# The order of one engine around the last score block of a head, and a weight block that is loaded in two halves

## The chip, the cores and the metric

The kernel runs on one core of a Trainium2 chip. The metric is the device time of one execution in microseconds (us). The times before are the median of three runs; one further execution was profiled, and the trace that is read here is of that one.

## What is computed

One pre-norm decoder block on 528 tokens (16 learned meta tokens and 512 tokens), width 1024, in float32. Two mixers run on the same normalised input `u`: a gated linear recurrence (HGRN2) and a differential softmax attention. Each has 8 heads of width 128. Cut to what matters for this change:

```
proj = u @ w_in                       # 10 blocks of 1024 columns; 8 of them are split over 8 heads
hq, hf, hi, hz, aq, ak, av, az, ga, gb = split(proj)
oA = rmsnorm(hgrn2(hq, log f, 1 - f, hi)) * silu(hz)      # per head
p  = softmax(q1 k1^T / 8) - lam * softmax(q2 k2^T / 8)    # causal, in 4 blocks of 128 queries
oB = rmsnorm(p @ v) * silu(az)                            # per head
m  = sigmoid(ga) * (oA @ w_a) + sigmoid(gb) * (oB @ w_b)
out = rmsnorm(h + m @ w_out)
```

## The kernel before, in words

**Products in three passes.** A float32 product is made of three passes in a faster format: each operand is split into a high part and a rest, and TensorE adds high x high, rest x high and high x rest (`three`, L639 to L641). So each weight block that arrives in `w_raw` needs a high part `w_hi`, written by ScalarE (ACT), and a rest `w_lo`, written by VectorE (DVE) or, for some blocks, by ScalarE and a DMA that adds (issued from GpSimd, POOL).

**A head.** The 8 heads run one after the other; heads 0 to 6 have the same program, the last (head 7) differs at its end. TensorE walks 60 slots in a fixed order. Slots 0 to 31 are four "units" of 8 slots (columns HI, HZ, AV, AZ of `w_in` for this head). Slots 32 to 59 are two "pairs" `r = 0, 1` of seven "parts" `j = 0..6` (two slots each): a Strassen-like scheme makes, of weight blocks for the *next* head (HF and HQ, then AK and AQ), sums of halves (`sum_2`, `sum_4` on DVE, and two adding DMAs, `add_s1` and `add_s3`), and DVE combines the products (`sum_75`, `sum_16`, `out_21`, `out_22`, `out_12`). Between the slots lie the small products of this head's recurrence and attention, at places written out by hand (`HG_AT`, `AT_AT`): the scores of the last query block `s3` after slot 44, the turned (transposed) probabilities `t3` after slot 51 (L892, L895), the product with the values `a3` after slot 53 (L901, L902), and `turn` after slot 59 (L846).

**The last score block.** It goes PE `s3`, DVE `masked(3)` (L1728, L1735: mask, negate, row minimum), ACT `exps(3)` (L1147), DVE `probs(3)` (L1745 to L1747), PE `t3`, ACT `probs_out(3)`, PE `a3`.

**The end of a head.** ACT `square` (L1139) of what `a3` left, DVE `norm_sum(1)` (L1672, L1677), POOL `rstd_pow` (L592), DVE `norm(1)` (L1684), PE `turn`. Then DVE `sum_16(1)` (L1525) and `out_21(1)` (L1546, the first that writes `qT`); TensorE may start the next head's first unit only when `out_21(1)` is done, since it overwrites the bank that `out_21` reads (the wait on `comb` in `unit`). `opening(h + 1)` (L1450 to L1457) prepares the next head's recurrence, and `half_hi`, `half_lo` (L334, L339) split the next head's first weight block HI.

**Queues.** Every engine works its list in order; a wait at its head holds all that is behind it. SyncE (SP) issues all loads: HI into `w_raw[0]` when the last rest of pair 1 (`low(1, 6)`) is done, then HZ into `w_raw[1]`; AV into `w_raw[0]` waits for `lo_ready`, the second half of HI's rest. POOL issues the adding DMAs and makes the power of -1/2 (`rstd_pow`).

After the heads six "gate" pairs follow; the first needs `add_s1` and `add_s3` on blocks GA and GB that are loaded in head 7. `add_s3` is issued by POOL behind the last `rstd_pow`.

Of the kernel before, what the change touches and what calls it, by code (L numbers as in the profile page):

```python
# [26 lines left out]
P = 128  # L27
# [4 lines left out]
KT = D // P  # L32
# [18 lines left out]
BLK = 512  # L51
SLOTS = 8
RAW = 2
UNITS = 4
# [53 lines left out]
def build(nc, x, meta_tokens, norm_g, w_in, lb_logits, hg_norm_g, da_lambda, da_norm_g,  # L108
# [124 lines left out]
    x_loaded = [sem(f"x_loaded{i}") for i in range(CH)]  # L233
    xres_loaded, stored = sem("xres_loaded"), sem("stored")
    w_loaded = [sem(f"w_loaded{i}") for i in range(2 * RAW)]

    slot_free = sem("slot_free")
    hi_ready, lo_ready, w_used = sem("hi_ready"), sem("lo_ready"), sem("w_used")
    hi_first = sem("hi_first")
    sums, pair_hi, pair_lo = sem("sums"), sem("pair_hi"), sem("pair_lo")  # L240
    base_loaded = [sem(f"base_loaded{i}") for i in range(2)]
    s1_added, s3_added, adds_begun = sem("s1_added"), sem("s3_added"), sem("adds_begun")
# [86 lines left out]

    def half_hi(act, half, loads, free):  # L330

        act.wait_ge(w_loaded[0], 16 * loads)
        act.wait_ge(w_used, free)
        act.activation(blk(w_hi, half), w_raw[:, 0, half * BLK:(half + 1) * BLK], ACT.Copy)             .then_inc((hi_first, hi_ready)[half], 1)  # L334

    def half_lo(dve, half, ready):

        dve.wait_ge((hi_first, hi_ready)[half], ready)
        ins = dve.tensor_tensor(blk(w_lo, half), w_raw[:, 0, half * BLK:(half + 1) * BLK], blk(w_hi, half).bitcast(F32),  # L339
                                ALU.subtract)  # L340
        if half == 1:
            ins.then_inc(lo_ready, 1)

    def part_hi(act, q, j, r, loads, i, free):

# [75 lines left out]
    with block:  # L421

        @block.sync
        def _(sp):
# [4 lines left out]
            def columns(h, col, r):  # L429

                load(r, w_in[bass.ds(h + col // P, 1), :, :])

            def base_21(h, col, r):

                sp.dma_start(sum_at(r), w_in[bass.ds(h + col // P, 1), :, 0:BLK].rearrange("u p n -> p (u n)")) \
                    .then_inc(base_loaded[r // RAW], 16)
# [10 lines left out]
            def pair_of_head(h, r, h_next, cols):  # L447

                q = 2 * h + r
                if r == 0:  # L450
                    base_21(h_next, cols[1], 0)
                    sp.wait_ge(unit_added[1], 16 * h + 16)
                    sp.sem_inc(slot_free, 1)
                else:
                    sp.wait_ge(sums, 2 * q - 1)
                    sp.wait_ge(pair_lo, LOWS * (q - 1) + 3)
                    sp.sem_inc(slot_free, 1)
                    base_21(h_next, cols[1], 0)
                    sp.wait_ge(pair_lo, LOWS * q)
                    sp.sem_inc(slot_free, 1)  # L460
                columns(h_next, cols[0], 0)
                if r == 0:
                    sp.wait_ge(unit_added[2], 16 * h + 16)
                else:
                    sp.wait_ge(part_added[1], 16 * q)
                sp.sem_inc(slot_free, 1)
                columns(h_next, cols[1], 1)
# [24 lines left out]
            with sp.Fori(0, HEADS - 1) as h:  # L492
                units_of_head(h)
                pair_of_head(h, 0, h + 1, PAIRS[0])
                pair_of_head(h, 1, h + 1, PAIRS[1])
                sp.wait_ge(pair_lo, LOWS * 2 * (h + 1))
                sp.sem_inc(slot_free, 1)
                columns(h + 1, HI, 0)
                sp.wait_ge(part_added[1], 32 * h + 32)
                sp.sem_inc(slot_free, 1)  # L500
                columns(h + 1, HZ, 1)
# [134 lines left out]
        def _(pe):  # L636
# [56 lines left out]

            def unit(h, j, k):

                if k == 0:
                    if j == 0:
                        pe.wait_ge(lo_ready, UNITS + h + 1)
                        pe.wait_ge(c11_taken, 2 * h + 2)
                    else:  # L700
                        pe.wait_ge(unit_added[j - 1], 16 * h + 16)
                    if j < 2:
                        pe.wait_ge(comb, 10 * h + 8 + 2 * j)
                    elif j == 2:
                        pe.wait_ge(sec_taken, UNITS + 2 * h + 1)
                    else:
                        pe.wait_ge(gate_ready, 2 * h + 3)
                section(4 + j, j, [k])
# [295 lines left out]
        def _(act):  # L1004
# [137 lines left out]
            def exps(h, b):  # L1142
                act.wait_ge(nb_ready, 4 * h + b + 1)
                n = n_keys(b)
                for comp in range(2):
                    e, at_nb = (e1, e2)[comp][:, b % 2, 0:n], 2 * (b % 2) + comp
                    act.activation(e, e, ACT.Exp, bias=nb[:, at_nb:at_nb + 1], scale=-1.0,  # L1147
                                   accum_out=(l_1, l_2)[comp][:, b:b + 1]).then_inc(exp_done, 1)
# [23 lines left out]
            def head(h, last):  # L1172
# [15 lines left out]
                def p_1(r):  # L1188

                    save_p1(2 * h + r, made(h, 2 * UNITS + PARTS * r))  # L1190

                def p_5(r):

                    save_p5(2 * h + r, made(h, 2 * UNITS + PARTS * r + 1))

                def parts(r, *js):

                    for j in js:
                        part_of_head(h, r, j)
# [31 lines left out]
                c_11(0)  # L1231
                parts(1, 0, 3)
                probs_out(h, 2)
                parts(1, 1, 2, 4, 5)
                exps(h, 3)
                if last:
                    gate_rest(0, 2 * h)
                else:
                    act.wait_ge(comb, 10 + 10 * h + 5)
                    act.activation(kk[:, META + HALF:], kk[:, META + HALF:], ACT.Tanh, scale=0.5).then_inc(k_tanh, 1)  # L1240
                p_1(1)
                p_5(1)
                parts(1, 6)
                probs_out(h, 3)
                square(h, 1, B_A, at_done, atn(h, "a3"))
                c_11(1)
                if last:
                    gate_hi(0, 0, 3)
                else:
                    half_hi(act, 0, UNITS * h + 7, made(h, 16))  # L1250
                    half_hi(act, 1, UNITS * h + 7, made(h, 17))
                    unit_hi(act, 1, UNITS * h + 7, 1, made(h, 19), True)

# [83 lines left out]
        def _(dve):  # L1337
# [128 lines left out]
            def first_chain(ins):  # L1466
                first_mark(ins)
                dve.wait_ge(dve_own, first[0])

            opening(0, first_mark, first_chain)  # L1470
            dve.sem_inc(dve_own, OWN - first[0])

# [81 lines left out]
            def head(h, last):  # L1554
# [257 lines left out]
                sum_16(0)  # L1812
                out_21(0)
                out_22(0)
                low(1, 1, 2)
                sum_2(dve, 2 * h + 1, 0)
                out_12(0)
                masked(3)
                sum_4(dve, 2 * h + 1, 0)
                low(1, 5)  # L1820
                probs(3)
                low(1, 6)
                sum_75(1)
                if not last:
# [2 lines left out]
                if last:  # L1827
                    gate_low(0, 0, 3)
                else:
                    half_lo(dve, 0, h + 1)  # L1830
                    half_lo(dve, 1, UNITS * h + UNITS + 5)
                norm(1, B_A)
                sum_16(1)
                out_21(1)
                out_22(1)
                gated(1)
                out_12(1)
# [143 lines left out]
```

## Time and profile before

| | us |
|---|---|
| median of 3 runs | 736.97 (735.65 to 739.42) |
| profiled execution, its own time | 736.84 |
| its span, from the first to the last instruction | 735.0 |
| TensorE busy with matmuls | 707.4 (96%) |
| VectorE busy | 531.7 (72%) |
| ScalarE busy | 364.4 (50%) |
| GpSimd busy | 111.9 (15%) |
| mean granted TensorE clock | 0.997 of full |

The profiled execution took 1.84 us more than its span (736.84 - 735.0), and 0.13 us less than the median. Busy times are sums over all instructions of an engine. A row of a timeline gives start, duration, engine, line, operation, tiles and shapes, and in brackets how long the engine had been idle before it and what it waited for. Matmuls overlap: one is started each 0.12 us or so although one lasts 0.28, so a short stall shows as a wider step between two starts rather than as idle time.

### The profile page before, as it was taken

How to read it: one execution, taken by the hardware profiler on the slowest of the kernel's cores; microseconds unless marked ns; L12 is line 12 of the kernel's file. 1: busy time of each engine (PE TensorE's matmuls, PEld its weight loads, DVE VectorE, ACT ScalarE, POOL GpSimd, SP SyncE). 2: the span in 40 equal slices, each digit the busy share in tenths (PEclk: the TensorE clock that was granted, in tenths of full speed). 3: DMA queues.
4: the chain of work that ended last, by engine and by line, in shares of the span. 5: the costliest groups of instructions: out<-in, count | busy, mean ns of one | idle time of the engine just before them, and what ended most of it. 6: DMA issues, size and time to landing. Idle time of an engine off the chain costs nothing.

```text
span 735.0 us, 14431 instructions
## 1 busy us (share of the span) xinstructions
PE 707.4 (96%) x4953; PEld 651.5 (89%) x4953; DVE 531.7 (72%) x1240; ACT 364.4 (50%) x739; POOL 111.9 (15%) x134
## 2 busy tenths in 40 slices
PE   3999999999999999999999999999989999999995
PEld 2998999999899999899989999989889988888884
DVE  4899888788778778868868877887678872735352
ACT  5454653655564555376455555446466562222232
POOL 2011211221121121121112112112111000000000
PEclk9999999999999999999999999999999999999998
DMA  7355546547547555654754655565747553335102
GB/s 271 115 130 129 129 123 164 129 114 177 111 111 194 120 128 138 162 127 123 164 139 101 188 107 134 143 166 127 196 124 207 189 174 112 98 103 201 58 13 102
DMA packets 35955, 101.86 MB, mean 139 GB/s; under 512 B 4018, under 2 KB 4420, under 8 KB 35924
## 3 DMA queue, kind: packets, MB, share of 16 engines
q1 hardware_dynamic: 21204, 68.29, 26.6%
q0 software_dynamic: 14400, 32.51, 25.6%
q10 hardware_dynamic: 320, 0.66, 0.3%
q8 instruction: 18, 0.29, 0.2%
q14 instruction: 13, 0.11, 0.0%
HBM read 66.84 MB, written 2.10 MB: 94 GB/s over the span
## 4 chain that ended last, share of the span: by engine, by line
PE 77%; DVE 7%; issue 6%; DMA 5%; ACT 2%; POOL 1%; DVEq 0%; SPq 0%; POOLq 0%; ACTq 0%
PE ps L639 21%; PE ps L641 21%; PE ps L640 21%; PE ps L805 3%; DMA w_raw<-w_raw 3%; PE ps L875 2%; PE ps L791 1%; PE ps L901 1%; DMA w_raw<-in_w_in 1%; PE ps L892 1%; PE ps L821 1%; DVE e L1735 1%; DMA x_in<-in_x 1%; ACT e L1147 1%; DVE e L1747 1%
## 5 line engine op out<-in xcount | busy, mean ns | idle before, releaser
L639 PE MATMUL ps<-uT_hi,w_hi 128*128 128x272 f32 (+3 forms) x704 | 226.3, 321 | 0.8 <-ACT p L1117 0.8
L640 PE MATMUL ps<-uT_lo,w_hi 128*128 128x272 f32 (+3 forms) x704 | 215.5, 306 | 0.0
L641 PE MATMUL ps<-uT_hi,w_lo 128*128 128x272 f32 (+3 forms) x704 | 215.2, 306 | 0.0
L639 PEld LDWEIGHTS ps<-uT_hi,w_hi 128*128 128x128 f32 x704 | 133.2, 189 | 8.6 <-issue 1.2
L641 PEld LDWEIGHTS ps<-uT_hi,w_lo 128*128 128x128 f32 x704 | 133.0, 189 | 6.0
L640 PEld LDWEIGHTS ps<-uT_lo,w_hi 128*128 128x128 f32 x704 | 133.2, 189 | 4.5
L639 PE MATMUL ps<-t_hi,w_hi 128*128 128x256 f32 x352 | 103.1, 293 | 2.6 <-DVE w_lo L362 2.6
L641 PE MATMUL ps<-t_hi,w_lo 128*128 128x256 f32 x352 | 99.5, 283 | 0.0
L640 PE MATMUL ps<-t_lo,w_hi 128*128 128x256 f32 x352 | 99.4, 282 | 0.0
L321 ACT ACTIVATE w_hi<-w_raw 128x1024 fp32r<-128x1024 f32 x53 | 56.0, 1059 | 84.2 <-PE ps L641 54.7
L355 ACT ACTIVATE w_hi<-w_raw 128x512 fp32r<-128x512 f32 x132 | 78.5, 624 | 21.9 <-DMA w_raw<-w_raw 9.0
L362 DVE TENSOR_TENSOR w_lo<-w_raw,w_hi 128x512 fp32r<-128x512 f32 x100 | 67.1, 687 | 11.2 <-ACT w_hi L355 9.8
L328 DVE TENSOR_TENSOR w_lo<-w_raw,w_hi 128x1024 fp32r<-128x1024 f32 x29 | 35.5, 1223 | 54.5 <-ACT w_hi L321 54.5
L1147 ACT ACTIVATE e<-e,small 128x144 f32<-128x144 f32 (+3 forms) x64 | 36.2, 566 | 74.5 <-DVE small L1735 74.5
L639 PEld LDWEIGHTS ps<-t_hi,w_hi 128*128 128x128 f32 x352 | 67.0, 190 | 5.3 <-DVE w_lo L362 3.0
L640 PEld LDWEIGHTS ps<-t_lo,w_hi 128*128 128x128 f32 x352 | 67.0, 190 | 0.0
L641 PEld LDWEIGHTS ps<-t_hi,w_lo 128*128 128x128 f32 x352 | 67.0, 190 | 0.0
L587 POOL DMA_DIRECT2D w_lo<-w_raw x32 | 31.9, 997 | 93.6 <-ACT w_lo L357 91.8
L564 POOL DMA_DIRECT2D w_lo<-w_raw x24 | 21.2, 885 | 132.0 <-ACT w_lo L323 132.0
L592 POOL TENSOR_TENSOR small<-small 128x4 f32<-128x4 f32 x16 | 17.5, 1094 | 118.8 <-DVE small L1677 63.8
L581 POOL DMA_DIRECT2D w_sum<-w_raw x22 | 19.3, 875 | 106.6 <-DMA w_raw<-in_w_in 99.3
L805 PE MATMUL ps<-qq,sq 128*128 128x128 f32 x192 | 29.3, 275 | 0.4 <-DVE sq L1638 0.4
(240 smaller groups left out, 1436.8 us busy)
## 6 DMA issues: line engine op xcount, KB each, us to landing
w_raw<-in_w_in SPq DMA_DIRECT2D x80, 512.0 KB, 3.4
w_lo<-w_raw POOLq DMA_DIRECT2D x24, 512.0 KB, 4.7
w_lo<-w_raw POOLq DMA_DIRECT2D x32, 256.0 KB, 4.3
w_sum<-in_w_in SPq DMA_DIRECT2D x22, 256.0 KB, 3.0
w_sum<-w_raw POOLq DMA_DIRECT2D x22, 256.0 KB, 3.3
w_raw<-w_raw POOLq DMA_DIRECT2D x22, 256.0 KB, 4.3
w_raw<-in_w_branch_a SPq DMA_DIRECT2D x8, 512.0 KB, 3.6
w_raw<-in_w_branch_b SPq DMA_DIRECT2D x8, 512.0 KB, 3.3
```

The lines of the kernel that those rows point to most:

```text
L321: act.activation(w_hi[:, slot, :], raw_at(r), ACT.Copy).then_inc(hi_ready, 1)
L328: eng.tensor_tensor(w_lo[:, slot, :], raw_at(r), w_hi[:, slot, :].bitcast(F32), ALU.subtract).then_inc(ready, 1)
L355: act.activation(blk(w_hi, i), part_src(r, j), ACT.Copy).then_inc(pair_hi, 1)
L362: dve.tensor_tensor(blk(w_lo, i), part_src(r, j), blk(w_hi, i).bitcast(F32), ALU.subtract).then_inc(pair_lo, 1)
L564: pool.dma_start(w_lo[:, slot, :], raw_at(r), accum_op=ALU.add).then_inc(unit_added[n], 16)
L581: pool.dma_start(sum_at(r), raw_at(r + 1)[:, BLK:], accum_op=ALU.add).then_inc(s1_added, 16)
L587: pool.dma_start(blk(w_lo, i), part_src(r, j), accum_op=ALU.add).then_inc(part_added[j - 3], 16)
L639: pe.matmul(dst, w[0], rhs[0], start=start, stop=False, skip_group_check=True)
L640: pe.matmul(dst, w[0], rhs[1], start=False, stop=False, skip_group_check=True)
L641: return pe.matmul(dst, w[1], rhs[0], start=False, stop=stop, skip_group_check=True)
L805: mm = pe.matmul(walk(dst, i * P // 2, (P, 2), (m, P // (2 * m)), (1, m)), k_mix[:, i, :], walk(qq[:, i * P:], m, (HALF - m, 2), (2 * m, P ...
L1147: act.activation(e, e, ACT.Exp, bias=nb[:, at_nb:at_nb + 1], scale=-1.0, accum_out=(l_1, l_2)[comp][:, b:b + 1]).then_inc(exp_done, 1)
```

## The change

Seven places, all in the heads:

- SP loads HI in two DMAs of 256 KB. The first is issued when `low(1, 5)` is done (one rest earlier than before), the second when `low(1, 6)` is done. Each half has a semaphore of its own.
- ACT `half_hi(0)` waits for the first half alone.
- DVE marks the rest of the first half (`lo_first`); TensorE starts the next head with that, and waits for the second half's rest (`lo_ready`) at slot 4 of the unit.
- DVE after `out_22(0)`: before `low(1, 1)`, `low(1, 2)`, `sum_2`, `out_12(0)`, `masked(3)`, `sum_4`, `low(1, 5)`, `probs(3)`, `low(1, 6)`; after `low(1, 1)`, `masked(3)`, `out_12(0)`, `low(1, 2)`, `sum_2`, `probs(3)`, `sum_4`, `low(1, 5)`, `low(1, 6)`.
- ACT: `exps(3)` goes ahead of `parts(1, 5)`; `p_1(1)`, `p_5(1)` and `parts(1, 6)` go ahead of the tanh (`gate_rest` in the last head).
- ACT: `c_11(1)` goes ahead of `square`.
- DVE: `half_lo(1)` goes from ahead of `norm(1)` to behind `out_21(1)`.

```diff
     def half_hi(act, half, loads, free):
 
-        act.wait_ge(w_loaded[0], 16 * loads)
+        act.wait_ge((half_loaded, w_loaded[0])[half], 16 * loads)
...
-        if half == 1:
-            ins.then_inc(lo_ready, 1)
+        ins.then_inc((lo_first, lo_ready)[half], 1)
...
+            def half_columns(h, col, half):
+
+                cols = slice(half * BLK, (half + 1) * BLK)
+                return sp.dma_start(w_raw[:, 0, cols],
+                                    w_in[bass.ds(h + col // P, 1), :, cols].rearrange("u p n -> p (u n)"))
...
+                sp.wait_ge(pair_lo, LOWS * 2 * (h + 1) - 1)
+                sp.sem_inc(slot_free, 1)
+                half_columns(h + 1, HI, 0).then_inc(half_loaded, 16)
                 sp.wait_ge(pair_lo, LOWS * 2 * (h + 1))
                 sp.sem_inc(slot_free, 1)
-                columns(h + 1, HI, 0)
+                half_columns(h + 1, HI, 1).then_inc(w_loaded[0], 16)
...
+                if (j, k) == (0, KT // 2):
+                    pe.wait_ge(lo_ready, UNITS + h + 1)
                 if k == 0:
                     if j == 0:
-                        pe.wait_ge(lo_ready, UNITS + h + 1)
+                        pe.wait_ge(lo_first, h + 1)
...
-                parts(1, 1, 2, 4, 5)
+                parts(1, 1, 2, 4)
                 exps(h, 3)
+                parts(1, 5)
+                p_1(1)
+                p_5(1)
+                parts(1, 6)
                 if last:
                     gate_rest(0, 2 * h)
...
-                p_1(1)
-                p_5(1)
-                parts(1, 6)
                 probs_out(h, 3)
+                c_11(1)
                 square(h, 1, B_A, at_done, atn(h, "a3"))
-                c_11(1)
...
-                    half_hi(act, 0, UNITS * h + 7, made(h, 16))
+                    half_hi(act, 0, h + 1, made(h, 16))
...
-                low(1, 1, 2)
+                low(1, 1)
+                masked(3)
+                out_12(0)
+                low(1, 2)
                 sum_2(dve, 2 * h + 1, 0)
-                out_12(0)
-                masked(3)
+                probs(3)
                 sum_4(dve, 2 * h + 1, 0)
                 low(1, 5)
-                probs(3)
                 low(1, 6)
...
                     half_lo(dve, 0, h + 1)
-                    half_lo(dve, 1, UNITS * h + UNITS + 5)
                 norm(1, B_A)
                 sum_16(1)
                 out_21(1)
+                if not last:
+                    half_lo(dve, 1, UNITS * h + UNITS + 5)
                 out_22(1)
```

## Rows read from the trace of the kernel before

**Rows 1.** The page: busy time, share and instructions of each engine.

```profile
PE 707.4 (96%) x4953; PEld 651.5 (89%) x4953; DVE 531.7 (72%) x1240; ACT 364.4 (50%) x739; POOL 111.9 (15%) x134
```

**Rows 2.** Waits of TensorE: us in total, times, longest.

```profile
PE ps L639 <- DVE w_lo L362: 2.6, 2, 2.0
PE ps L892 <- DVE e L1747: 1.2, 3, 0.6
```

**Rows 3.** Timeline of TensorE: turned probabilities in head 0, and in head 2.

```profile
97.70 0.66 PE L892 MATMUL ps<-ident,e 128*128 128x128 f32 x4 [0.58 <-DVE e L1747]
...
204.09 0.28 PE L641 MATMUL ps<-t_hi,w_lo 128*128 128x256 f32 x1
204.22 0.38 PE L892 MATMUL ps<-ident,e 128*128 128x128 f32 x2
...
218.33 0.28 PE L641 MATMUL ps<-t_hi,w_lo 128*128 128x256 f32 x1
218.75 0.66 PE L892 MATMUL ps<-ident,e 128*128 128x128 f32 x4
```

**Rows 4.** Timeline of VectorE around the last score block of head 2.

```profile
211.79 0.68 DVE L362 TENSOR_TENSOR w_lo<-w_sum,w_hi 128x512 fp32r<-128x512 f32 x1
...
213.02 0.68 DVE L370 TENSOR_TENSOR w_raw<-w_sum,w_raw 128x512 f32<-128x512 f32 x1
...
213.96 0.16 DVE L1728 CUSTOM_DVE_ANT_0 e<-ps,bias 128x16 f32<-128x16 f32 x1
...
218.83 0.69 DVE L362 TENSOR_TENSOR w_lo<-w_raw,w_hi 128x512 fp32r<-128x512 f32 x1
```

**Rows 5.** Timeline of ScalarE in the same stretch and at the head's end.

```profile
215.88 0.74 ACT L1147 ACTIVATE e<-e,small 128x528 f32<-128x528 f32 x1 [1.44 <-DVE small L1735]
...
222.16 0.60 ACT L1139 ACTIVATE sq<-ps 128x512 f32<-128x512 f32 x1 [1.87 <-PE ps L902]
...
223.21 1.16 ACT L334 ACTIVATE w_hi<-w_raw 128x512 fp32r<-128x512 f32 x2 [0.16 <-DMA w_raw<-in_w_in]
```

**Rows 6.** Timeline of TensorE: scores s3, pair 1's second part, head 2's end.

```profile
212.07 0.29 PE L865 MATMUL ps<-kT,qT 64*128 64x16 f32 x2
...
215.57 0.28 PE L639 MATMUL ps<-t_hi,w_hi 128*128 128x256 f32 x1
...
226.26 0.60 PE L846 MATMUL ps<-ident,st 128*128 128x128 f32 x4
226.62 0.39 PE L639 MATMUL ps<-uT_hi,w_hi 128*128 128x272 f32 x1
```

**Rows 7.** Timelines of GpSimd and VectorE at the ends of heads 2 and 3.

```profile
223.77 1.03 POOL L592 TENSOR_TENSOR small<-small 128x4 f32<-128x4 f32 x1 [8.91 <-DVE small L1677]
...
223.88 1.30 DVE L339 TENSOR_TENSOR w_lo<-w_raw,w_hi 128x512 fp32r<-128x512 f32 x2 [0.19 <-ACT w_hi L334]
...
284.29 1.57 POOL L592 TENSOR_TENSOR small<-small 128x4 f32<-128x4 f32 x1 [8.92 <-DVE small L1677]
...
284.27 1.29 DVE L339 TENSOR_TENSOR w_lo<-w_raw,w_hi 128x512 fp32r<-128x512 f32 x2
...
286.95 0.42 DVE L1546 TENSOR_TENSOR qT<-ps,p 128x256 f32<-128x256 f32 x1
```

**Rows 8.** Timeline of TensorE at the end of head 3.

```profile
286.77 0.60 PE L846 MATMUL ps<-ident,st 128*128 128x128 f32 x4
287.43 0.39 PE L639 MATMUL ps<-uT_hi,w_hi 128*128 128x272 f32 x1
```

**Rows 9.** The page's DMA issues: KB each, median us from issue to landing.

```profile
w_raw<-in_w_in SPq DMA_DIRECT2D x80, 512.0 KB, 3.4
...
w_sum<-in_w_in SPq DMA_DIRECT2D x22, 256.0 KB, 3.0
...
w_raw<-w_raw POOLq DMA_DIRECT2D x22, 256.0 KB, 4.3
```

**Rows 10.** The chain that ended last, behind head 7.

```profile
528.18 6.94 DMA w_raw<-w_raw
```

More of the change, by code:

```diff
@@ L235, in build @@
     w_loaded = [sem(f"w_loaded{i}") for i in range(2 * RAW)]
+    half_loaded = sem("half_loaded")
     slot_free = sem("slot_free")
     hi_ready, lo_ready, w_used = sem("hi_ready"), sem("lo_ready"), sem("w_used")
-    hi_first = sem("hi_first")
+    hi_first, lo_first = sem("hi_first"), sem("lo_first")
     sums, pair_hi, pair_lo = sem("sums"), sem("pair_hi"), sem("pair_lo")
@@ L1468, in first_chain @@
                 dve.wait_ge(dve_own, first[0])
+            dve.wait_ge(lo_ready, UNITS + 1)
+            dve.sem_inc(lo_first, 1)
             opening(0, first_mark, first_chain)
```

## The prediction

> **What bounds the kernel now.** I read the page first: TensorE is busy 96% of the span and the next engine, DVE, 72% [rows 1]. The page's clock line shows full speed but for the ends, so an edit of DVE's and ACT's order can only give back what TensorE loses in waiting. The view of waits gives 1.2 us in three waits for the turned probabilities `t3` (L892) and 2.6 us in two waits for a rest behind the last head [rows 2]. That list is short of the truth, since a stall hides in the overlap of matmuls. So the third view is TensorE's timeline, read by steps between starts. From the last product to the turned probabilities the step is 0.13 us where nothing is waited for, and 0.42 us at `t3` of head 2 [rows 3]: 0.29 lost. In head 0 the idle time of 0.58 and the 0.28 that the product before it lasts make a step of 0.86, so 0.73 lost [rows 3]. There are eight of these steps; head by head they lose 0.73, 0.27, 0.29, 0.26, 0.26, 0.42, 0.27 and 0.54, which is 2.50 in heads 0 to 6 and 0.54 in head 7. At the ends of heads 0 to 6 the next head's first product comes 0.36 behind the start of the turns (226.26 to 226.62) [rows 6], but 0.66 in head 3 [rows 8], 0.56 in head 5 and 0.38 in head 6: 0.30 + 0.20 + 0.02 = 0.52 lost. The rest of the idle time is at the kernel's start and behind head 7.
>
> **`masked(3)` and `probs(3)` earlier.** In head 2 TensorE's last score product starts at 212.07 and lasts 0.29 [rows 6], so the scores are there at 212.4. DVE starts `masked(3)` only at 213.96, behind `low(1, 1)` (211.79), `low(1, 2)`, `sum_2` (213.02) and `out_12(0)` [rows 4]. In the new order it stands behind `low(1, 1)`, which frees DVE at about 212.4 (its followers start 0.6 us after it), so it starts at 212.45, 1.5 earlier. From its start to `t3` took 218.75 - 213.96 = 4.79 [rows 3, 4], all of it one chain, since DVE had idle time before `probs(3)`; `exps(3)` loses its wait behind `parts(1, 5)`. So `t3` could start at 217.24. TensorE comes to it at 218.33 + 0.13 = 218.46: the stall goes, with 1.2 us to spare. Head 0 lies the same way. Gain: 2.50 in heads 0 to 6.
>
> What was ahead now comes later. `masked(3)` lasts at most 215.88 - 213.96 = 1.92 [rows 4, 5], so `out_12(0)` starts by 214.4 and ends by 214.8; TensorE's second part of pair 1 needs it at 215.57 [rows 6], 0.8 to spare. `low(1, 2)` is done by 215.5, and its part comes 12 steps of 0.12 behind 215.57, at 217.0. `sum_2` ends near 216, and ACT takes `parts(1, 5)` behind `exps(3)` with no loss. `probs(3)` ends at 217.2, `sum_4` and `low(1, 5)` take 0.6 each, to 218.4; `low(1, 6)` ends at 219.1, where it ended at 218.83 + 0.69 = 219.5 [rows 4]. The parts that use them come behind 222. I take nothing for all of these. If the 0.8 were used up, each 0.1 over it in a head would cost 0.7 in all.
>
> **HI in halves.** SP issues one DMA more per head. HZ, which stands behind it in SP's list, moves with `low(1, 6)`, some 0.4 earlier. A DMA of 256 KB from `w_in` lands in 3.0 us, one of 512 KB in 3.4 [rows 9]. The first half is issued near 218.6 and lands by 222.0; ACT reaches it right behind `square`. `square` started at 222.16 [rows 5] and now starts at 221.9, since `a3` moves with `t3`; `c_11(1)` fits in front of it, in what was 1.87 us of idle time [rows 5]. So `half_hi(0)` runs near 222.4 instead of 223.21 [rows 5]. TensorE had the whole HI rest 1.4 us before it started on it (223.88 + 1.30 = 225.2 against 226.62) [rows 6, 7]. The halves by themselves therefore give nothing. The second half's rest moves to about 226.4. TensorE needs it four slots of six 0.12 steps later, at 229.2 or after, so the new wait costs nothing. Nor do I price an extra wait instruction there: each part already begins with one, and its step is the usual 0.12. The load of AV waits for that rest, so it goes out 1.3 later. From an issue at 226.7 it takes 3.4 to land, two splits of about 1.1, and about 5.6 for the adding DMA, to 238; unit 2 begins 16 slots (11.5 us) and some 3 us of small products behind 226.3, at 240.8. Behind AV in SP's list is AZ, whose wait (the adding DMA on HZ) ends earlier than AV's. If this cover were gone it would cost up to 1.3 in each of seven heads.
>
> **The head's end, where I see the loss.** Count from the start S of `square`. Before, GpSimd's power starts at S + 1.61 (223.77) and takes 1.03. The two rests start 0.11 behind it and hold DVE until `norm(1)` at S + 2.93, 1.21 after they start [rows 5, 7]. In head 3 the first rest started at 284.27, 0.02 *before* the power (284.29), and the power took 1.57 [rows 7]; head 5 has the same, 0.09 before, with 1.49. The six other powers at a head's end take 1.03, and in none of them does a rest start first. `norm(1)` then starts at S + 3.13 to S + 3.21. `out_21(1)` is the last thing that TensorE waits for: 286.95 to 287.43 is 0.48 [rows 7, 8]. In the ordinary heads this 0.48 and the 0.36 behind the turns end together, so there is almost no slack, and the power's 0.5 cost TensorE 0.30 in head 3 and 0.20 in head 5. In the new kernel `half_hi(0)` is done at S + 1.1, before DVE finishes the mean (about S + 1.5), so `half_lo(0)` starts before the power in every head. Moving `half_lo(1)` away does not help, since the power holds `norm(1)`. I take head 5's 0.20 in all seven: 1.40, less the 0.52 that is there already: a loss of 0.88. Bounds: -0.52 (the power stays at 1.03; then `norm(1)` starts at S + 2.67 and all these stalls go) and 7 x 0.30 - 0.52 = 1.58.
>
> The Trainium skill says on the page "SBUF — State Buffer", section "Who interferes with whom", that a DVE instruction with two SBUF inputs contends with a GpSimd instruction that reads SBUF, and that the one that issues first keeps the shared port pair for its whole length. That speaks against this edit; the trace agrees in two heads (1.57 and 1.49 against 1.03). By the rule every head from 0 to 6 pays, which is the sum taken here; without it the sum would be the 733.2 of the first rival.
>
> **Behind head 7.** There `a3`, `square` and the power move 0.54 earlier, and `add_s3` stands behind that power. It took 6.94 us from issue to landing [rows 10], where the median is 4.3 [rows 9], and the first gate pair waits for it. The weight loads that it shares the DMA engines with go out about 1 us earlier too. So this stage gains between 0.54 and 0.54 + 2.6; if the adding DMAs met more traffic instead, it could gain nothing. I take 0.8, near the lower end, since most of that traffic remains.
>
> **Sum.** -2.50 + 0.88 - 0.8 = -2.42. From the profiled execution's own 736.84 that gives 734.4; the median of the runs is 0.13 above it, so 734.5.
>
> **Rivals.**
> 1. *The power isn't lengthened*, because one rest that is over early does less than the two. Then the loss of 0.88 becomes a gain of 0.52: 733.2. For it: six of eight powers are short. Against it: both long ones belong to rests that start first, and it is the first rest that overlaps.
> 2. *The traffic behind head 7 clears*: the stage gains 3.1 rather than 0.8, 732.2. For it: 6.94 against 4.3. Against it: the loads only move, they do not shrink.
> 3. *The stall moves.* `t3` is free, but another wait takes its 0.3 per head, `out_12(0)` for the second part or a longer wait at the head's end (0.30 instead of 0.20, and a tail of 0): about 736.5 to 737. For it: the slack at the head's end is nil. Against it: 0.8 spare at the second part.
> 4. *Slower: the first half of HI lands late.* `norm(1)` stands behind `half_lo(0)` on DVE. `half_lo(0)` may start by S + 2.5 (224.4) without cost, so the half must land by 223.8, 5.1 us after issue. Each us beyond costs 7 in all; from 6 us on it eats the gain and 3.7 more: 740.7 and above. Against it: 3.0 and 3.4 us for such loads.
>
> **Chances and range.** The forecast 0.56, rival 1 0.16, rival 2 0.10, rival 3 0.12, rival 4 0.06. About 0.5% (3.7 us: below 733.3, above 740.7) is what a measurement of this kernel can tell from no change. Rival 1 lies on that bound and counts half, rival 2 whole, and some of the forecast's own spread (a larger tail) lies below: faster 0.28. Slower 0.06, same 0.66. The forecast's own range is 733.5 to 735.5 (tail 0.54 to 1.5, head's end 0.5 to 1.58 of loss). The range that leaves out 2 in 10 reaches down to near rival 2 and up to no gain: 732.2 to 737.1.
>
> **What would show it.** `t3` (L892) comes 0.13 behind the product before it in all heads. `masked(3)` starts right behind the last score product. The powers at the end of heads 0 to 6 take about 1.5 with L339 starting first, and the first product of the next head comes 0.56 or so behind the turns. The first half lands before `square` ends. The last head's `add_s3` lands 0.5 to 1.5 earlier against the head's start. I am wrong if L892 still shows wide steps, if the powers stay at 1.03, or if a new wait stands in TensorE's list.

## The result, and the profile after

The changed kernel took 776.55 us (median of 4 runs, 774.97 to 778.45) against 737.08 for the kernel before in the same job: a ratio of 1.053, 95% interval 1.051 to 1.055. That is 39.5 us slower, where 734.5 and a range up to 737.1 were forecast. The profiled execution took 778.45 us, its span is 776.6 us and its mean granted clock 0.973.

First the page of the changed kernel: the same instructions, TensorE busy for 723.8 us instead of 707.4 [rows 1], and a clock line in which only a few of the nines have become eights.

```profile
PE 723.8 (93%) x4953; PEld 665.4 (86%) x4953; DVE 532.3 (69%) x1240; ACT 366.0 (47%) x739; POOL 113.5 (15%) x134
...
PEclk9999999999999899989989999999989999999998
...
w_raw<-in_w_in SPq DMA_DIRECT2D x73, 512.0 KB, 4.0
...
w_lo<-w_raw POOLq DMA_DIRECT2D x24, 512.0 KB, 6.2
```

The page of the kernel before has the row below for the last of these. By these medians the adding DMAs of 512 KB have become 1.5 us longer (6.2 against 4.7), and the loads 0.6 us longer (4.0 against 3.4 [rows 9]).

```profile
w_lo<-w_raw POOLq DMA_DIRECT2D x24, 512.0 KB, 4.7
```

TensorE's waits in the changed kernel (us in total, times, longest):

```profile
PE ps L886 <- DVE qT_lo L1728: 22.7, 6, 3.9
...
PE ps L648 <- DMA w_lo<-w_raw: 3.3, 7, 0.9
PE ps L648 <- DVE w_lo L362: 3.3, 1, 3.3
```

The wait for the turned probabilities [rows 2] has gone. A new one of 3.6 to 3.9 us stands in each of heads 1 to 6, in front of the *first* score block of the attention (L886, L875 before), a place that the change doesn't touch. From the turns at the end of head 0 to those of head 6 the kernel before needs 363.7 us (105.22 to 468.94), the changed one 402.2 (104.59 to 506.84): these six heads hold 38.5 of the 41.6 us that the span is longer.

In short, what the rows below show: AV, the block that goes into `w_raw[0]` behind HI, is loaded later. The DMA that adds on AV ends later still, and only then may HF, the next block for `w_raw[0]`, be loaded. ACT stands in its list before HF's split, and the split of `qT` behind it, which the first scores need, comes too late.

The text below counts from the start of the turns that end head 2: 226.26 before [rows 6], 237.25 after. All that follows is head 3's. TensorE after, at that point and at the stall:

```profile
229.66 0.28 PE L650 MATMUL ps<-t_hi,w_lo 128*128 128x256 f32 x1
229.78 0.60 PE L903 MATMUL ps<-ident,e 128*128 128x128 f32 x4
...
237.25 0.60 PE L857 MATMUL ps<-ident,st 128*128 128x128 f32 x4
237.74 0.39 PE L648 MATMUL ps<-uT_hi,w_hi 128*128 128x272 f32 x1
...
257.72 0.28 PE L650 MATMUL ps<-uT_hi,w_lo 128*128 128x264 f32 x1
...
261.92 0.85 PE L886 MATMUL ps<-kT,qT 64*128 64x144 f32 x4 [3.92 <-DVE qT_lo L1728]
```

The first pair is what the change was to bring: `t3` (L903) 0.12 behind the last product instead of 0.42 [rows 3]. The last row is the stall. To find its cause, follow the releasers back. DVE (first fence) waited 5.07 us for ACT's `qT_hi`; ACT (second fence) had that behind two splits (L355) that waited 7.15 us for a load from `w_in`:

```profile
234.59 0.69 DVE L340 TENSOR_TENSOR w_lo<-w_raw,w_hi 128x512 fp32r<-128x512 f32 x1
...
237.60 0.68 DVE L340 TENSOR_TENSOR w_lo<-w_raw,w_hi 128x512 fp32r<-128x512 f32 x1
...
261.18 0.69 DVE L1728 TENSOR_TENSOR qT_lo<-qT,qT_hi 128x512 fp32r<-128x512 f32 x1 [5.07 <-ACT qT_hi L1177]
```

```profile
258.48 1.15 ACT L355 ACTIVATE w_hi<-w_raw 128x512 fp32r<-128x512 f32 x2 [7.15 <-DMA w_raw<-in_w_in]
...
260.53 0.62 ACT L1177 ACTIVATE qT_hi<-qT 128x512 fp32r<-128x512 f32 x1
```

That load is HF, the first weight block of the pairs. SP's issues (first fence) and POOL's (second) show why it is late; the four loads are AV, AZ, `base_21` and HF, and the three adding DMAs (`add_unit`) work on HZ, AV and AZ:

```profile
238.53 0.33 SPq L427 DMA_DIRECT2D w_raw<-in_w_in  x1
244.90 0.33 SPq L427 DMA_DIRECT2D w_raw<-in_w_in  x1
245.42 0.33 SPq L441 DMA_DIRECT2D w_sum<-in_w_in  x1
252.61 0.33 SPq L427 DMA_DIRECT2D w_raw<-in_w_in  x1
```

```profile
234.77 1.40 POOL L601 TENSOR_TENSOR small<-small 128x4 f32<-128x4 f32 x1 [8.61 <-DVE small L1691]
...
238.93 0.92 POOL L573 DMA_DIRECT2D w_lo<-w_raw  x1 [2.76 <-ACT w_lo L324]
...
244.85 0.86 POOL L573 DMA_DIRECT2D w_lo<-w_raw  x1 [5.00 <-ACT w_lo L324]
...
251.90 0.86 POOL L573 DMA_DIRECT2D w_lo<-w_raw  x1 [6.19 <-ACT w_lo L324]
```

The same links in the kernel before: SP (AV, AZ, HF), POOL (the adding DMAs on HZ, on AV and on AZ), ACT (HF's split, `qT_hi`), and TensorE's first scores, for which it does not wait.

```profile
225.42 0.33 SPq L427 DMA_DIRECT2D w_raw<-in_w_in  x1
...
232.51 0.33 SPq L427 DMA_DIRECT2D w_raw<-in_w_in  x1
...
237.17 0.33 SPq L427 DMA_DIRECT2D w_raw<-in_w_in  x1
```

```profile
227.68 0.92 POOL L564 DMA_DIRECT2D w_lo<-w_raw  x1 [2.88 <-ACT w_lo L323]
...
231.44 0.85 POOL L564 DMA_DIRECT2D w_lo<-w_raw  x1 [2.84 <-ACT w_lo L323]
...
240.95 0.86 POOL L564 DMA_DIRECT2D w_lo<-w_raw  x1 [8.66 <-ACT w_lo L323]
```

```profile
240.41 1.21 ACT L355 ACTIVATE w_hi<-w_raw 128x512 fp32r<-128x512 f32 x2
...
242.99 0.63 ACT L1166 ACTIVATE qT_hi<-qT 128x512 fp32r<-128x512 f32 x1 [0.36 <-DVE qT L1709]
```

```profile
246.12 0.39 PE L875 MATMUL ps<-kT,qT 64*128 64x144 f32 x2
```

Side by side, in us from the turns:

| link | before | after | later by |
|---|---|---|---|
| AV load issued | -0.84 | +1.28 | 2.1 |
| adding DMA on AV issued | +5.18 | +7.60 | 2.4 |
| it is done, HF load issued | +10.91 | +15.36 | 4.5 |
| adding DMA on AZ issued | +14.69 | +14.65 | 0.0 |
| HF's split starts | +14.15 | +21.23 | 7.1 |

A load that goes out 2.1 us later ends in a split that comes 7.1 us later. The difference is made at two places.

- *The adding DMA on AV* takes 5.73 us before (5.18 to 10.91) and 7.76 after. SP sends AZ when the adding DMA on HZ is done. That was 1.07 us behind the start of the adding DMA on AV (231.44, 232.51); now the two go out 0.05 apart (244.85, 244.90), because AV's chain came 2.4 later and HZ's only 1.4. The 1.4 itself is an overlap: the adding DMA on HZ (227.68 before, 238.93 after) holds AZ's load for 5.97 us instead of 4.83, with AV's load going out 0.40 ahead of it instead of 2.26. From issue to landing it takes 4.5 to 4.6 us in heads 1 to 6 of every kernel here whose AV load goes out 0.5 us or more ahead of the turns, 4.7 to 5.5 where that load goes out 0.07 to 0.50 behind them, and 5.4 to 6.9 where it is 0.8 or more (experiment 5, with a load on either side, has 4.8 to 6.1).
- *HF's load* had landed before the adding DMA on AZ went out (240.41 against 240.95). Now it goes out 0.71 *behind* it (251.90, 252.61) and needs 5.9 us to the split instead of at most 3.2.

How much of this was spare is in the same rows. From the split's start to the scores are 3.44 us (258.48 to 261.92), and undelayed TensorE comes to the scores 19.86 behind the turns (226.26 to 246.12 in the kernel before). So the split may start as late as +16.4. It stood at +14.15, with 2.3 us to spare. The load's 2.1 alone would have fitted in; the 7.1 do not.

Last the windows over the stall (busy time of PE, PEld, DVE, ACT, POOL; then granted clock, DMA share, GB/s):

```profile
258.00:262.00 4.00, 0.08 (x3) 0.08 (x2) 0.82 (x2) 2.67 (x5) 0.00 (x0) 0.79 0.38 131
262.00:264.00 2.00, 2.00 (x13) 1.75 (x14) 1.77 (x6) 0.00 (x0) 1.92 (x3) 0.50 0.28 48
264.00:266.00 2.00, 2.00 (x11) 2.00 (x10) 0.00 (x0) 0.00 (x0) 0.71 (x1) 0.50 1.05 176
266.00:268.00 2.00, 2.00 (x11) 1.79 (x11) 0.58 (x2) 0.00 (x0) 0.00 (x0) 0.71 1.00 169
268.00:270.00 2.00, 2.00 (x12) 1.62 (x11) 1.95 (x12) 0.74 (x4) 0.00 (x0) 1.00 0.00 0
```

After 3.9 us without a matmul TensorE works at a granted clock of 0.50 (1.2 of 2.4 GHz) until about 267: 2.0 us lost in the two full windows and 0.58 in the one at 0.71, together 2.6. Read in the same way in slices of 1 us, the six stalls cost 1.7, 1.7, 2.6, 2.9, 3.2 and 1.7, in sum 13.8. With the waits of 22.7 that is 36.5 of the 38.5.

### The profile page after: what moved, and what is told of

Same layout as the page of the kernel before. It is cut to its first block and busy times, and to the rows that moved or that the text cites. A ratio compares the mean times of both kernels' runs of the same rounds, so it can differ in the third digit from the quotient of the medians.

```text
span 776.6 us, 14466 instructions
## 1 busy us (share of the span) xinstructions
PE 723.8 (93%) x4953; PEld 665.4 (86%) x4953; DVE 532.3 (69%) x1240; ACT 366.0 (47%) x739; POOL 113.5 (15%) x134
## 3 DMA queue, kind: packets, MB, share of 16 engines
q0 software_dynamic: 14400, 32.51, 23.9%
## 5 line engine op out<-in xcount | busy, mean ns | idle before, releaser
L648 PE MATMUL ps<-uT_hi,w_hi 128*128 128x272 f32 (+3 forms) x704 | 231.1, 328 | 3.3 <-DMA w_lo<-w_raw 3.3
L649 PE MATMUL ps<-uT_lo,w_hi 128*128 128x272 f32 (+3 forms) x704 | 218.9, 311 | 0.0
L650 PE MATMUL ps<-uT_hi,w_lo 128*128 128x272 f32 (+3 forms) x704 | 218.4, 310 | 0.0
L648 PEld LDWEIGHTS ps<-uT_hi,w_hi 128*128 128x128 f32 x704 | 137.0, 195 | 14.7 <-issue 7.5
L650 PEld LDWEIGHTS ps<-uT_hi,w_lo 128*128 128x128 f32 x704 | 136.4, 194 | 6.1
L649 PEld LDWEIGHTS ps<-uT_lo,w_hi 128*128 128x128 f32 x704 | 136.7, 194 | 4.3
L355 ACT ACTIVATE w_hi<-w_raw 128x512 fp32r<-128x512 f32 x132 | 78.1, 624 | 62.8 <-DMA w_raw<-in_w_in 48.2
L573 POOL DMA_DIRECT2D w_lo<-w_raw x24 | 21.2, 884 | 134.0 <-ACT w_lo L324 134.0
L601 POOL TENSOR_TENSOR small<-small 128x4 f32<-128x4 f32 x16 | 19.5, 1217 | 114.5 <-DVE small L1691 59.9
L816 PE MATMUL ps<-qq,sq 128*128 128x128 f32 x192 | 31.1, 287 | 0.5 <-DVE sq L1652 0.5
```

The lines of the kernel that those rows point to most:

```text
L355: act.activation(blk(w_hi, i), part_src(r, j), ACT.Copy).then_inc(pair_hi, 1)
L573: pool.dma_start(w_lo[:, slot, :], raw_at(r), accum_op=ALU.add).then_inc(unit_added[n], 16)
L601: pool.tensor_tensor(rstd[:, 0:CH], ms[:, 0:CH], half_neg[:, 0:CH], ALU.pow).then_inc(rstd_ready, 1)
L648: pe.matmul(dst, w[0], rhs[0], start=start, stop=False, skip_group_check=True)
L649: pe.matmul(dst, w[0], rhs[1], start=False, stop=False, skip_group_check=True)
L650: return pe.matmul(dst, w[1], rhs[0], start=False, stop=stop, skip_group_check=True)
```

## The experiments

Ten kernels, each timed against the kernel before on the same chip (in the first of three jobs that took 738.06, in the second 737.42, in the third 737.68). Theory A: the late load of AV does it. The rivals: the load of HI in two DMAs (theory B in the expectations), or the new orders of DVE and ACT (theory C). Issue times are given from the start of the turns, for heads 1 to 6; waits and windows are those of each kernel's profiled execution.

**1. The late rest alone** (on the kernel before; TensorE starts on the first half as in the change):

```diff
-                    half_lo(dve, 1, UNITS * h + UNITS + 5)
                 norm(1, B_A)
                 sum_16(1)
                 out_21(1)
+                if not last:
+                    half_lo(dve, 1, UNITS * h + UNITS + 5)
```

> The kernel before with one edit: the second half of HI's rest is made behind out_21(1) instead of ahead of norm(1), TensorE starts a head on the first half's rest and waits for the second at slot 4. HI still comes in one DMA, no other order is changed. Theory A (the later rest sends AV's load out some 2 us later, it collides with the adding DMAs, HF comes late, ACT's list stands before the qT split, TensorE waits 3.9 us for the first scores in heads 1 to 6 and then runs a while at the low clock): 770 to 780 us. Theory B (the halves of HI and their small packets are what costs): 735 to 738. Theory C (the new orders of DVE and ACT around the last score block cost): 735 to 738.

780.10 us, ratio 1.057 (1.055 to 1.060). AV goes out at +0.89 to +1.51, and TensorE waits 22.1 us for `qT_lo` in seven waits. One moved instruction makes the whole loss; neither HI in halves nor the orders around the last score block are in it.

**2. The whole change but for that rest:**

```diff
                     half_lo(dve, 0, h + 1)
+                    half_lo(dve, 1, UNITS * h + UNITS + 5)
                 norm(1, B_A)
                 sum_16(1)
                 out_21(1)
-                if not last:
-                    half_lo(dve, 1, UNITS * h + UNITS + 5)
```

> The changed kernel with that one edit undone: the second rest is made ahead of norm(1) again, all else as changed. Theory A: the wait for the first scores (L886) goes in all heads, 733 to 736 us, and the step to the turned probabilities stays at 0.12 us. Theories B and C: 770 to 778 us, as the changed kernel.

736.37 us, ratio 0.997 (0.995 to 0.998), 0.4 above the range of theory A and far from the others. AV goes out at -1.13 to -0.73. One wait for the first scores is left where none was expected (0.7 us, in head 2; see experiment 9). With experiment 1 this places the loss from both sides.

**3. The orders of DVE and ACT alone**, on the kernel before:

```diff
-                low(1, 1, 2)
-                sum_2(dve, 2 * h + 1, 0)
-                out_12(0)
+                low(1, 1)
                 masked(3)
+                out_12(0)
+                low(1, 2)
+                sum_2(dve, 2 * h + 1, 0)
+                probs(3)
                 sum_4(dve, 2 * h + 1, 0)
                 low(1, 5)
-                probs(3)
```

(and ACT's list as in the change).

> The kernel before with only the new orders of DVE around masked(3) and of ACT around exps(3) and c_11(1); HI in one DMA, both rests ahead of norm(1). Theory A: 733 to 735 us, the 2.5 us in heads 0 to 6 and some 0.8 behind head 7 are gained. Theory C: 760 us or more. Theory B: as A here.

737.52 us, ratio 1.000 (0.998 to 1.002): no loss, so theory C falls, but not the gain to 733 to 735 that was expected either. AV goes out at -0.74 to -0.51. The `t3` stall has gone in all eight heads (a step of 0.12). The rows of the end of head 2 show where half of that gain went: POOL, then DVE, then TensorE.

```profile
223.33 1.03 POOL L592 TENSOR_TENSOR small<-small 128x4 f32<-128x4 f32 x1 [8.58 <-DVE small L1678]
```

```profile
223.66 1.29 DVE L339 TENSOR_TENSOR w_lo<-w_raw,w_hi 128x512 fp32r<-128x512 f32 x2 [0.41 <-ACT w_hi L334]
224.87 0.68 DVE L1685 TENSOR_TENSOR st<-ps,small 128x512 f32<-128x512 f32 x1
...
225.92 0.42 DVE L1547 TENSOR_TENSOR qT<-ps,p 128x256 f32<-128x256 f32 x1
```

```profile
225.82 0.60 PE L846 MATMUL ps<-ident,st 128*128 128x128 f32 x4
226.40 0.39 PE L639 MATMUL ps<-uT_hi,w_hi 128*128 128x272 f32 x1
```

The power and `square` come earlier, but HI's load, the splits and the two rests do not, and `norm(1)` stands behind both rests. So `out_21(1)` is late by the time that the turns have gained: the next head begins 0.58 behind the turns instead of 0.36 [rows 6], and 0.53 to 0.71 in the other heads. Over heads 0 to 6 this gives back 1.3 of the 2.5. Up to the last turns 1.5 us are won (528.68 against 530.21), behind them 0.3 are lost.

**4. The load alone**, with no engine's order changed: in the kernel before SP also waits for `out_22(1)` of the head before (`comb` counts DVE's combining instructions).

```diff
                 sp.wait_ge(lo_ready, UNITS + h + 1)
+                sp.wait_ge(comb, 10 * h + 9)
                 sp.sem_inc(slot_free, 1)
                 columns(h, AV, 0)
```

> The kernel before with one wait more in SP's list and nothing else: the load of AV also waits until out_22(1) of the head before is done, which is 1.7 us after the second rest and 0.9 us after the turns start, where the changed kernel issues it 1.3 us after. No engine's order changes. Theory A: the load's time is all that matters, so a wait for the first scores shows in heads 1 to 6 and the time is 750 to 777 us. Theories B and C: 736 to 738 us.

780.07 us, ratio 1.055 (1.051 to 1.059), 3 us above the 750 to 777 that theory A gave. AV at +0.83 to +1.18, HF at +14.9 to +15.9, its split at +20.8 to +21.4:

```profile
PE ps L876 <- DVE qT_lo L1715: 22.9, 6, 4.0
```

The issue time of one load is enough; DVE's new order at the head's end is not needed for the loss.

**5. AV in halves**, on the changed kernel: the first half as soon as the first rest is done, the second as before.

```diff
+                sp.wait_ge(lo_first, h + 1)
+                half_columns(h, AV, 0).then_inc(av_half, 16)
                 sp.wait_ge(lo_ready, UNITS + h + 1)
                 sp.sem_inc(slot_free, 1)
-                columns(h, AV, 0)
+                half_columns(h, AV, 1).then_inc(w_loaded[0], 16)
...
+                act.wait_ge(av_half, 16 * h + 16)
                 unit_hi(act, 0, UNITS * h + 4, 2, made(h - 1, 21), True)
```

> The changed kernel with AV's load in halves too: the first 256 KB go out when HI's first rest is done (lo_first), some 2.5 us before the turns' end, the second when the second rest is done, as in the changed kernel. Theory A (AV's bytes meet the adding DMA on HZ's slot, AZ and HF follow late): half of the bytes move ahead, AV lands earlier by about 1 us, and HF's load comes back towards +11 us; the first scores wait less or not at all: 735 to 760 us. If only the second half's issue matters, as a rival to it: 770 to 778 us.

773.05 us, ratio 1.048 (1.045 to 1.051): a miss for the 735 to 760 of theory A; the rival of that expectation, that only the second half's issue matters, gave 770 to 778. The first half goes out at -1.79, but the second at +1.27 to +1.35, and both splits of AV and its adding DMA wait for the second. HF goes out at +14.2 to +15.1, little earlier, and the split stays at +20.1 to +20.5, with 21.2 us of waits.

**6. What the late load blocks.** HF is not needed by the scores; it only stands ahead of `qT_hi` in ACT's list. On the changed kernel:

```diff
-                parts(0, 0, 3)
                 take(h, 5)
                 rotated_hi(h, 1)
+                parts(0, 0, 3)
```

> The changed kernel with one edit on ACT: take(5) and the split of qT go ahead of the splits of HF's block, whose load comes late. The loads stay as late as in the changed kernel. Theory A, its last link (ACT's list stands before HF and holds the qT split): the wait for the first scores (L886) goes, TensorE's clock stays at its high level there, and the time is 735 to 745 us. Rival (qT itself is late, or DVE is): the wait stays, 770 to 778 us.

740.83 us, ratio 1.005 (1.004 to 1.007). The loads are as late as in the changed kernel (HF +15.1 to +15.6, split +20.5 to +21.5), yet no wait for `qT_lo` is left, and the clock is at 0.996. ACT in head 3, whose turns are at 226.82:

```profile
243.68 0.63 ACT L1177 ACTIVATE qT_hi<-qT 128x512 fp32r<-128x512 f32 x1 [1.32 <-DVE qT L1723]
...
248.36 1.15 ACT L355 ACTIVATE w_hi<-w_raw 128x512 fp32r<-128x512 f32 x2 [4.05 <-DMA w_raw<-in_w_in]
```

So the path from the late load to TensorE is this one place in ACT's list. What is left of it is a wait of 2.3 us in six heads for the adding DMA on AV, which unit 2 needs.

**7. The rest in between**, behind `norm(1)`, on the changed kernel:

```diff
                 norm(1, B_A)
+                if not last:
+                    half_lo(dve, 1, UNITS * h + UNITS + 5)
                 sum_16(1)
                 out_21(1)
-                if not last:
-                    half_lo(dve, 1, UNITS * h + UNITS + 5)
```

> The changed kernel with the second rest right behind norm(1), two instructions earlier than in it. AV's load goes out near 0.4 us after the turns start, instead of 1.3 us after and 0.8 us before in the kernel before. Theory A as a cliff between the two: anything from 740 to 776 us, with a wait for the first scores in some or all of heads 1 to 6, shorter than 3.9 us. Theory of a plain delay (each us of the load costs one): 737 to 745 us.

755.26 us, ratio 1.024 (1.021 to 1.027), within the 740 to 776 of theory A and outside the 737 to 745 of a plain delay. AV at +0.49, HF at +14.0 to +14.4, split at +18.3 to +20.1, 13.3 us of waits in six. The edit also has a cost of its own: `sum_16(1)` and `out_21(1)` now stand behind the second rest, and TensorE waits 3.6 us in seven for `out_21(1)`.

**8. The best guess**: the rest early again, as in 2, and AV in halves, as in 5.

> The second rest ahead of norm(1) as in e2, and AV's load in halves as in e5, all else as changed. AV's first half goes out about 1.3 us before its second. Theory A: no wait for the first scores in any head (e2 has 0.7 us in one), HF early; 733 to 736.5 us, at or below e2.

735.22 us, ratio 0.998 (0.996 to 0.999). AV's halves go out at -1.78 and about -1.1, HF at +9.5 to +11.9, no wait for the scores, as expected. Each against the kernel before in its job, this one (0.998) and experiment 2 (0.997) cannot be told apart, and both lie within the prediction's bound of 0.5%.

**9. A smaller dose of the load alone**: as 4, but SP waits for two steps less of DVE (`comb` 10 * h + 7).

> As e4, the kernel before with one wait more in SP's list, but for an event 0.8 us earlier (sum_16(1) done): AV's load goes out about 0.1 us after the turns start, where before it is 0.9 us ahead, in e7 0.5 us and in e4 about 1.1 us behind. Theory A with a steep rise between -0.9 and +0.5: between 738 and 752 us, with waits for the first scores that are shorter than e7's 2.2 us. If the load had slack up to some point between this and e7: 736 to 738 us. If any lateness costs in full: 770 us or more.

754.35 us, ratio 1.025 (1.021 to 1.028), 2 us above the 738 to 752 that was expected. AV at +0.07 to +0.29, HF at +13.7 to +14.1, its split at +18.1 to +18.7:

```profile
PE ps L876 <- DVE qT_lo L1715: 11.0, 6, 2.0
```

The limit of +16.4 worked out above gives waits of 1.7 to 2.3 for these splits; measured are 1.5 to 2.0, 1.8 in the mean. In the one head of experiment 2 in which AZ followed within 0.47 us, the split came at +17.34 and the scores waited 0.73.

**10. The adding DMA on AZ held back** until HF has landed, on the changed kernel:

```diff
                 add_unit(h, 1, 0, 2)
+                pool.wait_ge(w_loaded[0], 64 * h + 80)
                 add_unit(h, 2, 1, 3)
```

> The changed kernel with one wait more on GpSimd: the third adding DMA (AZ's slot, 512 KB) is issued only when HF's load has landed, so that the two no longer run side by side. AV, AZ and HF are issued as late as in the changed kernel. Theory A's collision: HF then lands 3.2 to 3.8 us after its issue instead of 5.9, the wait for the first scores falls from 3.9 to about 1.5 us, 748 to 762 us; unit 3, which needs that adding DMA, has room for it. Rival (HF's load is slow for another reason, such as its own queue): 774 to 780 us.

756.46 us, ratio 1.026 (1.022 to 1.029). HF goes out as late as in the changed kernel (+14.9 to +16.0). ACT's split in head 3, whose turns are at 232.54 and whose HF load was issued at 247.76:

```profile
251.21 1.15 ACT L355 ACTIVATE w_hi<-w_raw 128x512 fp32r<-128x512 f32 x2 [4.73 <-DMA w_raw<-in_w_in]
```

So the load takes 3.45 us instead of 5.9; the waits for the scores fall from 22.7 to 8.7 us, and with them most of the time at the low clock. The wait for the adding DMA on AV stays (3.0 in six, with one for HZ's; 3.3 in seven in the changed kernel), and the last unit, which needs the DMA that was held back, doesn't wait. The price is in another place: the load of HQ, which goes into the buffer that this DMA reads, goes out at about +23.9 instead of +21.0 in head 3, ACT's splits stand before it, and TensorE waits 5.3 us in seven for `v_a`, which ACT copies behind them (0.8 in one in the changed kernel). In sum 20 of the 39.5 us come back; so this overlap holds at least half of the loss.

All kernels in which AV comes in one DMA and ACT's list and the adding DMAs are as in the changed kernel or the one before, by the issue of AV (heads 1 to 6):

| kernel | AV issued, us from the turns | HF's split | time, us |
|---|---|---|---|
| 2 | -1.13 to -0.73 | +13.9 to +17.3 | 736.4 |
| before | -1.06 to -0.84 | +13.8 to +14.5 | 737.1 |
| 3 | -0.74 to -0.51 | +14.3 to +16.4 | 737.5 |
| 9 | +0.07 to +0.29 | +18.1 to +18.7 | 754.4 |
| 7 | +0.49 | +18.3 to +20.1 | 755.3 |
| 4 | +0.83 to +1.18 | +20.8 to +21.4 | 780.1 |
| 1 | +0.89 to +1.51 | +19.6 to +21.4 | 780.1 |
| changed | +1.27 to +1.35 | +20.9 to +21.5 | 776.6 |

## Why the prediction was wrong

**The failed step is the cover of AV's load** in "HI in halves": "The load of AV waits for that rest, so it goes out 1.3 later. From an issue at 226.7 it takes 3.4 to land, two splits of about 1.1, and about 5.6 for the adding DMA, to 238; unit 2 begins [...] at 240.8", and "If this cover were gone it would cost up to 1.3 in each of seven heads." The sum took nothing for it. Three things in it did not hold.

- *It followed AV only to unit 2.* There its bound of 1.3 per head held: TensorE waits 3.0 us in six heads for that adding DMA (0.3 to 0.9 each). But the end of the same DMA also frees `w_raw[0]` for HF, HF's split heads ACT's list, and behind it stands `qT_hi`, for which the first scores wait. Experiments 4 (the load alone makes the loss) and 6 (ACT's order alone takes it away) show both ends of that chain.
- *It took DMA durations from the kernel before as fixed.* It gave the adding DMA on AV 5.6 us and its end +11.7 (238); it took 7.76 and ended at +15.36. By the old durations the load's delay would have passed into the 2.3 us that HF's split had spare. The transfers were long or short by what ran beside them, and the delay grew from 2.1 to 7.1. Experiment 10 shows one of the three overlaps by itself (HF beside the adding DMA on AZ); AZ beside the adding DMA on AV was read from 60 heads (below), AV beside the adding DMA on HZ in the same way, and neither was tried alone.
- *The delay itself was 2.1 and not 1.3.* The rest starts at +0.35, takes 0.68 and only then lets the load go.

And the bound "up to 1.3 in each of seven heads" left out that a long stall also costs clock: 13.8 us here.

**Point by point.** The `t3` stall: right in all heads (0.12), and worth its 2.50 where it was; but in experiment 3 half of it (1.3) came back as a wider step at the head's end, as the third rival described it. "Halves by themselves give nothing": experiment 2 agrees (736.4 with the halves, 737.5 without them in experiment 3); as the two differ in other ways, no more is shown. The longer powers: right in all of heads 0 to 6, 1.40 to 1.41 with L340 starting 0.18 ahead (234.59, 234.77), but cheaper: the steps behind the turns are 0.48 to 0.57 (0.56 forecast), 0.5 us more than before in sum instead of 0.88. Where the power starts first, as in experiment 3 (223.33, the rest at 223.66), it takes 1.03. By the rule named in the prediction (the Trainium skill, "SBUF — State Buffer", "Who interferes with whom") this was to be expected, and the trace agrees.

**A second step failed, the one behind head 7.** Forecast was a gain of 0.8. From the last turns to the end of the span are 206.9 us (776.6 - 569.67) against 204.8 (735.0 - 530.21), a loss of 2.1. The prediction let the first gate pair wait for `add_s3`. The rows show it waiting for `add_s1`, the adding DMA on `w_sum`, which does not stand behind the power. Before, then after, each with SP's load of `base_21`, POOL's `add_s1`, and ACT's split that waits for it:

```profile
516.97 0.33 SPq L435 DMA_DIRECT2D w_sum<-in_w_in  x1
...
524.65 0.86 POOL L581 DMA_DIRECT2D w_sum<-w_raw  x1 [6.62 <-DMA w_raw<-in_w_in]
...
532.85 0.63 ACT L355 ACTIVATE w_hi<-w_sum 128x512 fp32r<-128x512 f32 x1 [4.10 <-DMA w_sum<-w_raw]
```

```profile
559.42 0.33 SPq L441 DMA_DIRECT2D w_sum<-in_w_in  x1
...
566.36 0.86 POOL L590 DMA_DIRECT2D w_sum<-w_raw  x1 [8.31 <-DMA w_raw<-in_w_in]
...
573.66 0.63 ACT L355 ACTIVATE w_hi<-w_sum 128x512 fp32r<-128x512 f32 x1 [5.45 <-DMA w_sum<-w_raw]
```

From the last turns, `add_s1` went out at -5.56 and goes out at -3.31, and its split has moved from +2.64 to +3.99. TensorE's first gate product follows at +4.05 and +5.40, after a wait of 3.3 us (2.0 before), and the granted clock is 0.50 from 575 to 581. The start of it is a term that was taken as nothing: `sum_2` now comes later, and in head 7 SP loads `base_21` when it is done, at -10.25 instead of -13.24. The 512 KB load that `add_s1` needs goes out at -9.2 in both, but with `base_21` only 1.06 ahead it takes 5.31 us instead of 3.14. It takes 5.4 to 5.9 in experiments 2, 3 and 8 too, with `base_21` 0.9 ahead. That the nearness makes it long is read from these five traces and was not tried. The sign named for this stage failed as well: `add_s3` lands at +5.22 instead of +4.91.

**The slower rival** (the first half of HI late) did not happen: no wait of TensorE is for a half of HI. The other signs named as "what would show it" came true, and "a new wait stands in TensorE's list" is what proved it wrong.

Experiment 2 is what the prediction described in all but the rest's place: 736.4, inside the range that was given, 1.7 us below the kernel before in its job where 2.4 were forecast. That is in part luck. In its trace the turns that end head 6 come 1.68 us earlier than before (467.26 against 468.94), close to the forecast 2.50 - 0.88 = 1.62; but from there to the end it loses 2.1 instead of gaining 0.8.

## What to carry to other kernels

When an edit delays a load, follow its buffer through every reuse, to the load that comes next in the same buffer and to whatever stands behind *that* load's consumer in its engine's list. Compare the spare time at the end of the chain with a delay that includes the new overlaps: look at which transfers start between the old and the new issue time, since a transfer's duration in the old trace holds only beside its old neighbours. And in an in-order list, put the work that waits for a far transfer behind the work that doesn't, as in experiment 6.

## What was not expected of the hardware

- Transfers of one core slow each other, and most of the effect comes within half a us of distance. Taken over heads 2 to 6 of all twelve traces (60 heads); a 256 KB load (`base_21`) follows AZ's by 0.5 us each time:

| what goes out, and how far behind what | heads | takes, us |
|---|---|---|
| AZ's load from 0.06 ahead to 0.48 behind the adding DMA on AV (the time is that of the adding DMA) | 42 | 7.45 to 7.93 |
| the same, 0.69 and 0.74 behind | 2 | 6.68, 6.47 |
| the same, 0.95 to 1.95 behind | 16 | 5.04 to 5.74 |
| HF's load 2.7 or more ahead of the adding DMA on AZ (the time is HF's, to its split) | 23 | at most 3.2 to 3.8 |
| the same, 0.59 and 0.25 ahead | 2 | at most 3.3, 3.9 |
| the same, 0.35 to 0.44 behind | 6 | 4.2 to 4.7 |
| the same, 0.57 to 1.4 behind | 29 | 5.2 to 6.0 |

- So the time does not grow evenly with the issue: from -1.0 to -0.6 (experiment 3) nothing is lost, between there and +0.2 lie 17 us, and from +0.2 to +1.0 it is 26 more (754.4 and 780.1 in experiments 9 and 4, which differ in the load alone). Experiment 7 lies between them at 755.3, but it has the changed kernel's other edits and a wait of its own, so it is no point of the same curve. What in the DMA engines makes this was not looked into.
- TensorE, stopped for about 3.9 us in the middle of a busy stretch, came back at 0.50 of its clock in head 3 and stayed there until about 5 us after it had resumed. Shorter stalls did the same, but not each time: the granted clock fell to 0.50 for 3.4 us at four of the six stalls of 1.5 to 2.0 us in experiment 9 (after waits of 1.8 to 2.0, and not after another of 1.8), and in experiment 7 at the waits of 2.8 in heads 5 and 6, but not at those of 2.7 and 2.9 in heads 2 and 4. It fell at none of the six of 1.3 to 1.6 us in experiment 10, nor in the heads of experiment 6, which has no such wait.
